# The low part of each weight slot on GpSimd: eight instructions of 256 columns instead of one of 2048

## The chip, the cores and the metric

The kernel runs on one core of one Trainium2 chip. The metric is the device time of one execution in microseconds, the median of three runs. Times inside an execution come from one profiled execution and are given in microseconds from its first instruction.

## What is computed

The reference is a stack of four transformer-like layers over a sequence of 512 tokens with 1024 features, all in float32. Cut to what matters here:

```python
def first_block(x, ...):                       # DEPTH = 2
    h = rms_norm(x, g_mix[0])
    x = x + rwkv7_time_mix(h, ...)             # products with w1, a1, k, r, g1, v, g2, o
    x = x + swiglu_ffn(rms_norm(x, g_ffn[0]), ffn_w_gu[0], ffn_w_down[0])
    k_sh, v_sh = shared_kv(x, kv_g, kv_w, ...)
    x = x + diff_attention(rms_norm(x, g_mix[1]), k_sh, v_sh, ...)
    x = x + swiglu_ffn(rms_norm(x, g_ffn[1]), ffn_w_gu[1], ffn_w_down[1])

def second_block(x, ...):
    x = _even_layer(x, w_in, ..., w_out, ...)  # gated linear attention and spatial gating
    x = _odd_layer(x, w_in, ..., w_out, ...)   # retention and multi-scale pooling
```

The feed-forward part has a gate and up weight of 1024 x 5632 and a down weight of 2816 x 1024 in each of two layers. Together with the projections of the four layers these weights are read once, 143 MB, and every product is computed with the 512 tokens at once.

## The kernel before

**Split products.** A matmul of this kernel takes its operands in a rounded float32 format. To keep float32 precision each operand is split into a high part (the rounded copy) and a low part (original minus high part), and a product is three matmuls: high by high, low by high, high by low (lines 2227, 2228 and 2229, the helper `three`). Activations are in `X_hi` and `X_lo`, eight tiles of 128 x 512.

**Weight slots.** All weights pass through a stream of 135 slots, each of 128 partitions x 2048 columns of float32 (8 tiles of 128 rows by 256 output features; some are smaller). Slot n uses buffer n % 2 of `weight_raw`, `w_hi` and `w_lo`. Four engines hand it on:

- SyncE loads `weight_raw` (1 MB in two DMAs) once the low part of slot n - 2 is made (`lo_ready`).
- ScalarE copies it to `w_hi` (`high`, line 1110), once the DMA has landed (`raw_full`) and TensorE has gone through slot n - 2 (`kstep`), and counts up `hi_ready`.
- GpSimd subtracts: `w_lo = weight_raw - w_hi` (`low`, line 989), and counts up `lo_ready`.
- TensorE waits for `lo_ready` at the first matmul of the slot (`features` and `tokens`). A slot gives 48 matmuls of 128 x 128 by 512 columns.

`regions(n, t)` gives the parts of a slot that hold weights: one part in nearly all, two in slot `g2`, where the first is linked to the second by a wait (`link`). It is two-dimensional for a full slot (`t[:, :]`) and three-dimensional for some narrower ones.

**Order.** Each engine runs its own list of instructions, written out by hand, in order. GpSimd's list is mostly `low` for slot after slot, in the order of the products. In between it has four subtractions for the decay sums of the first layer after each of three `k` slots (line 1017), the level masks of the state solver (lines 1031 and 1038), the gate products of the even layer (line 1050) and the window sums of the odd layer (line 1068). ScalarE's list mixes `high` with the activations, evictions of PSUM and the copies to `X_hi` (line 1128). In the feed-forward loop (`ffn` in each engine's part; two slots an iteration, eleven iterations, for each layer) ScalarE makes the high part of the next slot, then the gate (`Silu`, line 1095), then the high part of the hidden tile (line 1097). VectorE takes the products out of PSUM (lines 1659 and 1660), multiplies them (1663) and makes the low part of the hidden tile (1666).

**VectorE elsewhere.** Around the slots VectorE prepares the activations: `xf` from the normalised state by a scalar product and sum (line 1740), from `x` by a gain (line 1637), and `X_lo = xf - X_hi` (line 1610). Other lines named below: 1802, a running sum along the tokens; 1810, one small scaling; 1961 to 1973, the norm and rotation of queries and keys; 2027 to 2038, the decays of the even layer; 2077, a low part of an inverse norm; 2093, a layer norm's gain; 1696, the subtraction of a mean.

Of the kernel before, what the change touches and what calls it, by code (L numbers as in the profile page):

```python
# [14 lines left out]
F32 = mybir.dt.float32  # L15
# [3 lines left out]
ALU = mybir.AluOpType  # L19
# [196 lines left out]
def step_end(s):  # L216
    return PL.kstart[s + 1]
# [277 lines left out]
def regions(n, t):  # L495

    name = PL.slots[n][0]
    v = t[:, :].rearrange("p (k c) -> p k c", k=8)
    if name in ("a1", "elr"):
        return [v[:, :, 0:128]]  # L500
    if name == "g1":
        return [v[:, :, 0:160]]
    if name == "a2":
        return [t[:, 0:1024]]
    if name == "g2":
        return [t[:, 0:1024], t[96:128, 1024:2048]]
    if name in ("dn0", "dn1") and PL.slots[n][1] % 3 == 2:
        return [v[:, 0:6, :]]
    return [t[:, :]]


def build(nc, t, out):

    JB = make_jobs()
    ctx = ExitStack()
    with ctx:
# [249 lines left out]
        def wait_done(eng, key):  # L766

            eng.wait_ge(job_done, JB.info[key][2] + 1)

        def wait_job(eng, key):  # L770

            _, who, _, n = JB.info[key]
            eng.wait_ge(job_a if who == "A" else job_d, n)
# [6 lines left out]
        def wait_product(eng, name):  # L780
            wait_step(eng, PL.first[name] + PL.count[name] - 1)
# [34 lines left out]
        def whole(tile):  # L816
            return tile[:, :, :, :].rearrange("p b k c -> p (b k) c")

        def mask(name, n=2 * KT):
            at_ = CORE_MASKS.index(name)  # L820
            return lvl[:, at_:at_ + 1, :].to_broadcast([P, n, CH])
# [152 lines left out]
        @block.gpsimd  # L974
        def _(pool):
            seq = [0]

            def link(ins):

                seq[0] += 1  # L980
                ins.then_inc(pool_seq, 1)
                pool.wait_ge(pool_seq, seq[0])

            def low(n, dyn=0):

                pool.wait_ge(hi_ready, n + 1 + dyn)
                parts = list(zip(regions(n, weight_raw[n % 2]), regions(n, w_hi[n % 2]), regions(n, w_lo[n % 2])))
                for i, (r, h, l) in enumerate(parts):
                    ins = pool.tensor_tensor(l, r, h.bitcast(F32), ALU.subtract)  # L989
                    if i < len(parts) - 1:  # L990
                        link(ins)
                ins.then_inc(lo_ready, 1)
                if len(parts) > 1:
                    pool.wait_ge(lo_ready, n + 1)

            def low_product(name):
                for i in range(sum(1 for q in PL.slots if q[0] == name)):
                    low(PL.first_slot[name] + i)

            def low_ffn(layer):  # L1000
                n0 = PL.first_slot[f"gu{layer}"]
                with pool.Fori(0, FT // 2) as i:
                    for j in range(2):
                        low(n0 + j, 2 * i)
                n0 = PL.first_slot[f"dn{layer}"]
                with pool.Fori(0, 2) as i:
                    for j in range(6):
                        low(n0 + j, 6 * i)

            for name in ("a1", "a2"):  # L1010
                low_product(name)
            low(PL.first_slot["k"])
            for i in range(1, 4):
                low(PL.first_slot["k"] + i)
                for k in range(4 * i - 4, min(4 * i, KT)):
                    pool.wait_ge(w_sum, k + 1)
                    pool.tensor_tensor(u0[:, k, :], rf[:, k, :], u0[:, k, :], ALU.subtract).then_inc(w_before, 1)
            for name in ("r", "g1", "v"):
                low_product(name)

            pool.wait_ge(kstep, step_end(PL.first["v"] + 3))
            for i in range(2):
                ins = pool.memset(state[i][:, :, :], 0.0)
            ins.then_inc(zero_ready, 1)
            pool.wait_ge(lvl_in, 16)
            for tt in range(TT):
                wait_job(pool, ("AtX", tt))
                for g in range(2):
                    for slot in range(2):
                        part = TT2[1][:, g, slot, 1, :, :]  # L1030
                        pool.tensor_tensor(part, part, mask("eye", 4), ALU.add).then_inc(f_ready, 1)
                pool.wait_ge(at_copied, tt + 1)
                for lv in range(2, NLV + 1):
                    if lv >= 3:
                        wait_done(pool, ("G", tt, lv - 2, 1))
                    elif tt:
                        wait_done(pool, ("G", tt - 1, 4, 1))
                    pool.tensor_tensor(whole(Lm[(lv + 1) % 2]), whole(At), mask(f"lv{lv}"),
                                       ALU.mult).then_inc(level_ready, 1)
            low_product("g2")  # L1040
            low_product("o")
            low_ffn(0)
            for name in ("q", "kk", "kv", "ao"):
                low_product(name)
            low_ffn(1)
            for name in ("eq", "ek", "elr", "ev", "esv", "eu", "egb", "ega"):
                low_product(name)
            wait_product(pool, "egb")
            for g in range(4):
                pool.tensor_tensor(mix[:, 4 + g, :], mix[:, 4 + g, :], egb[:, g, :], ALU.mult).then_inc(gate_p, 1)  # L1050
            low_product("eo")
            wait_product(pool, "eo")
            pool.memset(opp[:, :, 0:PAD], 0.0).then_inc(pad_p, 1)
            for name in ("oq", "ok", "ov", "op", "ogd"):
                low_product(name)

            pool.wait_ge(pad_p, 1)
            pool.wait_ge(rot_done, 4)
            link(pool.memset(psh[:, :, 0:PAD], 0.0))
            wait_product(pool, "op")  # L1060
            for g in range(4):
                if g >= 1:
                    pool.wait_ge(win_d, g)
                src = opp[:, g, :]
                for i in range(g + 1):
                    dst = psh[:, i % 2, :]
                    sh = 1 << i
                    ins = pool.tensor_tensor(dst[:, PAD:PAD + S], src[:, PAD:PAD + S],
                                             src[:, PAD - sh:PAD - sh + S], ALU.add)
                    if i < g:  # L1070
                        link(ins)
                    src = dst
                ins.then_inc(win_p, 1)
                if g in (1, 3):
                    low(PL.first_slot["ogc"] + g // 2)
            low_product("oo")
# [1811 lines left out]
```

## Time and profile before

| | |
|---|---|
| time, median of 3 runs | 2346.48 us (2332.41 to 2347.68) |
| time of the profiled execution | 2346.41 us |
| its span, first to last instruction | 2344.3 us |
| TensorE busy | 2075.5 us (89%) |
| TensorE weight loads | 1585.3 us (68%) |
| VectorE busy | 838.8 us (36%), 1217 instructions |
| ScalarE busy | 803.3 us (34%), 1043 instructions |
| GpSimd busy | 687.1 us (29%), 198 instructions |
| of it line 989 (`w_lo`) | 605.3 us, 136 instructions |
| read from HBM | 143 MB, mean 63 GB/s |
| mean granted TensorE clock | 0.927 of full speed |

Busy time of an engine counts from the start to the end of its instructions, including time in which an instruction is held. Durations of TensorE's matmuls overlap: while the busy time of one is 0.39 us, the next starts 0.23 us after it at full clock. PE is TensorE, PEld its weight loads, DVE VectorE, ACT ScalarE and POOL GpSimd. A line such as L989 is a line of the kernel.

### The profile page before, as it was taken

The page shows a single profiled execution, that of the slowest core. Times are in us where ns is not written, and L with a number is a line of the kernel's source. Part 1 is how long each engine was busy: PE and PEld are TensorE (multiplying, and loading weights), DVE is VectorE, ACT ScalarE, POOL GpSimd, SP SyncE. Part 2 cuts the span into 40 slices and gives each one's busy share as a digit, 9 for nine tenths or more (in the row PEclk, how much of TensorE's full clock was granted, in tenths as well). Part 3 has the DMA queues.
Part 4 walks back from the last instruction along what each step waited for, and adds up shares of the span by engine and source line. Part 5 has one row for each costly group of instructions (what it writes and reads, how often), then busy time and mean ns, then how long its engine had stood idle before and what let it go on. Part 6 is the DMA issues. An engine that isn't in the chain of part 4 may idle for free.

```text
span 2344.3 us, 36168 instructions
## 1 busy us (share of the span) xinstructions
PE 2075.5 (89%) x15556; PEld 1585.3 (68%) x15556; DVE 838.8 (36%) x1217; ACT 803.3 (34%) x1043; POOL 687.1 (29%) x198
## 2 busy tenths in 40 slices
PE   5979876667999999988997789999998999979997
PEld 2656856653778888866665467888887885747764
DVE  4876153333332221023656633222101234252333
ACT  5663332233244432132124434443212413232232
POOL 0333232201233344423310023334443423203430
PEclk7689999996799999999998789999999998889999
DMA  3112100001123332222210012333322211112110
GB/s 110 36 54 67 41 4 4 4 23 46 54 72 93 104 89 99 99 80 73 68 41 18 1 55 72 95 102 89 99 99 90 90 55 54 36 59 90 54 54 36
DMA packets 190702, 147.06 MB, mean 63 GB/s; under 512 B 6888, under 2 KB 188351, under 8 KB 190576
## 3 DMA queue, kind: packets, MB, share of 16 engines
q1 hardware_dynamic: 190576, 145.18, 20.1%
q8 instruction: 104, 1.70, 0.3%
q14 instruction: 22, 0.18, 0.0%
HBM read 143.06 MB, written 2.10 MB: 62 GB/s over the span
## 4 chain that ended last, share of the span: by engine, by line
PE 77%; DVE 9%; ACT 6%; issue 4%; POOL 2%; DMA 1%; SPq 0%; DVEq 0%; ACTq 0%
PE psum L2227 20%; PE psum L2229 19%; PE psum L2228 19%; PE psum L2376 4%; DVE X_lo L1610 2%; ACT w_hi L1110 1%; PE psum L2303 1%; POOL w_lo L989 1%; DVE xf L1740 1%; PE psum L2233 1%; PE psum L2638 1%; ACT xf L1142 1%; DVE col L2002 1%; PE psum L2601 1%; PE psum L2795 1%
## 5 line engine op out<-in xcount | busy, mean ns | idle before, releaser
L989 POOL TENSOR_TENSOR w_lo<-weight_raw,w_hi 128x2048 fp32r<-128x2048 f32 (+2 forms) x136 | 605.3, 4452 | 1433.3 <-ACT w_hi L1110 1433.1
L2227 PE MATMUL psum<-X_hi,w_hi 128*128 128x512 f32 x1544 | 644.2, 417 | 62.1 <-DVE X_lo L1610 42.5
L2229 PE MATMUL psum<-X_hi,w_lo 128*128 128x512 f32 x1544 | 617.4, 400 | 0.0
L2228 PE MATMUL psum<-X_lo,w_hi 128*128 128x512 f32 x1544 | 617.3, 400 | 0.0
L2227 PEld LDWEIGHTS psum<-X_hi,w_hi 128*128 128x128 f32 x1544 | 299.5, 194 | 181.5 <-issue 95.8
L1110 ACT ACTIVATE w_hi<-weight_raw 128x2048 fp32r<-128x2048 f32 (+2 forms) x136 | 251.7, 1850 | 381.2 <-PE psum L2229 369.8
L2228 PEld LDWEIGHTS psum<-X_lo,w_hi 128*128 128x128 f32 x1544 | 300.2, 194 | 64.6 <-issue 6.7
L2229 PEld LDWEIGHTS psum<-X_hi,w_lo 128*128 128x128 f32 x1544 | 299.3, 194 | 65.9
L1659 DVE TENSOR_TENSOR sgate<-rt,psum 128x512 f32<-128x512 f32 x44 | 30.2, 687 | 320.4 <-PE psum L2229 320.4
L2227 PE MATMUL psum<-hb_hi,w_hi 128*128 128x512 f32 x352 | 136.9, 389 | 0.0
L2228 PE MATMUL psum<-hb_lo,w_hi 128*128 128x512 f32 x352 | 136.9, 389 | 0.0
L2229 PE MATMUL psum<-hb_hi,w_lo 128*128 128x512 f32 x352 | 136.9, 389 | 0.0
L2227 PE MATMUL psum<-w_hi,X_hi 128*128 128x256 f32 x384 | 116.4, 303 | 12.6 <-DVE X_lo L1610 6.5
L1095 ACT ACTIVATE sgate<-sgate 128x512 f32<-128x512 f32 x44 | 27.9, 635 | 255.2 <-DVE sgate L1659 255.2
L2228 PE MATMUL psum<-w_lo,X_hi 128*128 128x256 f32 x384 | 111.0, 289 | 0.0
L2229 PE MATMUL psum<-w_hi,X_lo 128*128 128x256 f32 x384 | 110.9, 289 | 0.0
L1649 DVE TENSOR_TENSOR x<-x,psum 128x512 f32<-128x512 f32 x32 | 20.5, 682 | 224.2 <-PE psum L2229 224.2
L1610 DVE TENSOR_TENSOR X_lo<-xf,X_hi 128x512 fp32r<-128x512 f32 x88 | 76.3, 868 | 50.5 <-ACT X_hi L1128 49.0
L2227 PEld LDWEIGHTS psum<-w_hi,X_hi 128*128 128x128 f32 x384 | 76.3, 199 | 24.8 <-issue 21.8
L2228 PEld LDWEIGHTS psum<-w_lo,X_hi 128*128 128x128 f32 x384 | 76.4, 199 | 2.0 <-issue 1.9
L2229 PEld LDWEIGHTS psum<-w_hi,X_lo 128*128 128x128 f32 x384 | 76.1, 198 | 0.0
L2227 PEld LDWEIGHTS psum<-hb_hi,w_hi 128*128 128x128 f32 x352 | 66.1, 188 | 13.8
(426 smaller groups left out, 2639.2 us busy)
## 6 DMA issues: line engine op xcount, KB each, us to landing
weight_raw<-in_ffn_w_gu SPq DMA_DIRECT2D x88, 512.0 KB, 4.9
weight_raw<-in_l_w_in SPq DMA_DIRECT2D x45, 512.0 KB, 4.6
weight_raw<-in_ffn_w_down SPq DMA_DIRECT2D x40, 512.0 KB, 3.7
weight_raw<-in_kv_w SPq DMA_DIRECT2D x16, 512.0 KB, 4.1
weight_raw<-in_l_w_out SPq DMA_DIRECT2D x16, 512.0 KB, 4.1
weight_raw<-in_rw_w_k SPq DMA_DIRECT2D x8, 512.0 KB, 4.1
weight_raw<-in_rw_w_r SPq DMA_DIRECT2D x8, 512.0 KB, 4.0
weight_raw<-in_rw_w_v SPq DMA_DIRECT2D x8, 512.0 KB, 4.5
```

The costliest lines, as they stand in the source:

```text
L989: ins = pool.tensor_tensor(l, r, h.bitcast(F32), ALU.subtract)
L1095: act.activation(sgate[:, j, :], sgate[:, j, :], ACT.Silu).then_inc(ff_gate, 1)
L1110: last = act.activation(h, r, ACT.Copy)
L1142: act.activation(xf[:, i % 2, :], h_sb[:, k, 1:S + 1], ACT.Copy, scale=omu[:, 8 * mu + k:8 * mu + k + 1]).then_inc(mix_half, 1)
L1610: dve.tensor_tensor(X_lo[:, k, :], f, X_hi[:, k, :].bitcast(F32), ALU.subtract).then_inc(xlo_ready, 1)
L1659: dve.tensor_tensor(sgate[:, j, :], rt[:, :], bank(b[0]), ALU.mult).then_inc(ff_raw, 1)
L1740: return dve.scalar_tensor_tensor(out=f, in0=h_sb[:, k, 0:S], scalar=pcol("rw_mu", 8 * mu + k), in1=f, op0=ALU.mult, op1=ALU.add)
L2002: link(dve.tensor_reduce(col[:, 14:16], psum[:, b:b + 2, 0:N], AX.X, ALU.max))
L2227: pe.matmul(ps, wh, xh, start=start, stop=False, skip_group_check=True)
L2228: pe.matmul(ps, wh, xl, start=False, stop=False, skip_group_check=True)
L2229: return pe.matmul(ps, wl, xh, start=False, stop=stop, skip_group_check=True)
L2376: ins = pe.matmul(out(q, r, k), left(q, r, k), right(q, r, k), start=True, stop=True, skip_group_check=True)
```

## The change

`pieces` cuts a part of a slot: a three-dimensional part into its k tiles (8, or 6 in the last slot of a down product), a two-dimensional one into stretches of 256 columns. `low` goes through the pieces of a part one after the other and writes the same values. There is no wait between pieces, and the signal `lo_ready` is still given by the last instruction of the slot. A full slot has eight instructions of 128 x 256 instead of one of 128 x 2048; the slots of 128 or 160 columns per k tile have eight of that width, and those of 1024 columns four.

```diff
+def pieces(r):
+
+    if len(r.shape) == 3:
+        return [r[:, k:k + 1, :] for k in range(r.shape[1])]
+    return [r[:, c:c + 256] for c in range(0, r.shape[1], 256)]
@@
                 parts = list(zip(regions(n, weight_raw[n % 2]), regions(n, w_hi[n % 2]), regions(n, w_lo[n % 2])))
-                for i, (r, h, l) in enumerate(parts):
-                    ins = pool.tensor_tensor(l, r, h.bitcast(F32), ALU.subtract)
+                for i, part in enumerate(parts):
+                    for r, h, l in zip(*(pieces(q) for q in part)):
+                        ins = pool.tensor_tensor(l, r, h.bitcast(F32), ALU.subtract)
                     if i < len(parts) - 1:
                         link(ins)
                 ins.then_inc(lo_ready, 1)
```

## Rows read from the trace of the kernel before

**Rows 1.** The chain that ended last, shares of the span by line.

```profile
by line: PE psum L2227 20.3%; PE psum L2229 19.1%; PE psum L2228 19.1%; issue 4.2%; PE psum L2376 4.2%; DVE X_lo L1610 2.2%; ACT w_hi L1110 1.4%; PE psum L2303 1.4%; POOL w_lo L989 1.4%; DVE xf L1740 1.3%; PE psum L2233 0.9%; PE psum L2638 
```

**Rows 2.** The chain in order of time: start us, us, what; VectorE pieces.

```profile
146.32 4.50 DVE xf L1740
...
643.15 4.70 DVE X_lo L1610
...
1204.92 4.90 DVE tq L1969
...
1778.81 7.71 DVE X_lo L1610 x6
...
1961.52 2.97 DVE en_lo L2077
...
2072.01 2.35 DVE x L1696
```

**Rows 3.** Timeline, GpSimd and VectorE: start us, us, engine line op out<-in [idle before].

```profile
642.68 4.62 POOL L989 TENSOR_TENSOR w_lo<-weight_raw,w_hi 128x2048 fp32r<-128x2048 f32 x1 [6.29 <-ACT w_hi L1110]
...
1982.93 3.70 DVE L2093 TENSOR_SCALAR esv<-esv,pv 128x512 f32<-128x512 f32 x1
```

**Rows 4.** Waits, 671 to 913 us: waited for, us in total, times, longest us.

```profile
PEld psum L2227 <- POOL w_lo L989: 4.0, 10, 0.4
```

**Rows 5.** Timeline of the first feed-forward product, ScalarE, GpSimd and TensorE.

```profile
710.93 4.60 POOL L989 TENSOR_TENSOR w_lo<-weight_raw,w_hi 128x2048 fp32r<-128x2048 f32 x1 [7.96 <-ACT w_hi L1110]
...
729.67 1.28 ACT L1110 ACT_TABLE_LOAD   x1
730.97 1.92 ACT L1110 ACTIVATE w_hi<-weight_raw 128x2048 fp32r<-128x2048 f32 x1
732.96 4.60 POOL L989 TENSOR_TENSOR w_lo<-weight_raw,w_hi 128x2048 fp32r<-128x2048 f32 x1 [7.96 <-ACT w_hi L1110]
...
737.25 0.39 PE L2229 MATMUL psum<-X_hi,w_lo 128*128 128x512 f32 x1
737.62 0.50 PE L2227 MATMUL psum<-X_hi,w_hi 128*128 128x512 f32 x1
```

**Rows 6.** Timeline of GpSimd: instructions that follow each other, merged with their count.

```profile
102.97 8.69 POOL L1017 TENSOR_TENSOR u<-rf,u 128x512 f32<-128x512 f32 x4
...
252.78 9.04 POOL L989 TENSOR_TENSOR w_lo<-weight_raw,w_hi 128x2048 fp32r<-128x2048 f32 x2 [19.82 <-ACT w_hi L1110]
...
298.30 2.78 POOL L1031 TENSOR_TENSOR TT<-TT,lvl 128x256 f32<-128x256 f32 x4 [3.06 <-DVE TT L1841]
```

**Rows 7.** The chain in order of time: `w_lo`, first and last of seven.

```profile
117.96 4.66 POOL w_lo L989
...
2203.64 4.57 POOL w_lo L989
```

**Rows 8.** Timeline, GpSimd and TensorE: down product, and a slot of 1831.69.

```profile
926.82 4.61 POOL L989 TENSOR_TENSOR w_lo<-weight_raw,w_hi 128x2048 fp32r<-128x2048 f32 x1 [7.81 <-ACT w_hi L1110]
932.78 0.39 PE L2227 MATMUL psum<-hb_hi,w_hi 128*128 128x512 f32 x1
...
1831.69 5.39 POOL L989 TENSOR_TENSOR w_lo<-weight_raw,w_hi 128x2048 fp32r<-128x2048 f32 x1 [7.99 <-ACT w_hi L1110]
```

**Rows 9.** Timeline of TensorE: what ended its idle time, after three stalls.

```profile
1135.30 0.70 PE L2611 MATMUL psum<-aq,cst 128*128 128x512 f32 x1 [0.39 <-DVE aq L1961]
...
1212.10 0.70 PE L2611 MATMUL psum<-ak,cst 128*128 128x512 f32 x1 [1.68 <-DVE ak L1961]
...
1964.53 0.50 PE L2233 MATMUL psum<-en_hi,heads_r 16*128 16x512 f32 x1 [3.58 <-DVE en_lo L2077]
```

**Rows 10.** Stretches: us, busy us by engine (x count), PEclk, DMA share, GB/s.

```profile
120.00:124.00 4.00, 1.64 (x8) 1.06 (x7) 1.11 (x1) 3.54 (x7) 4.00 (x3) 1.00 0.05 14
...
152.00:158.00 6.00, 5.65 (x18) 4.30 (x18) 3.42 (x6) 3.73 (x6) 0.00 (x0) 0.72 0.45 157
...
1966.00:1976.00 10.00, 10.00 (x24) 7.04 (x24) 5.87 (x6) 0.63 (x1) 3.31 (x3) 0.53 0.25 85
```

## The prediction

> **What bounds the kernel now.** I read the chain that ended last by line, then in order of time, then the waits by stretch, and last the timeline of single engines around each place where the chain leaves TensorE. The three matmul lines of the split products alone are 58% of the chain [rows 1], so nothing outside TensorE counts unless TensorE waits for it. Two things that belong to this change do stand on the chain: `w_lo` on GpSimd with 1.4% (33 us, seven pieces of about 4.6 us) and `X_lo` on VectorE with 2.2%, although one `X_lo` takes 0.68 us when it is alone.
>
> The `X_lo` share is a stall by GpSimd. At 146.32, 643.15 and elsewhere on the chain a VectorE operation of 0.5 to 0.75 us lasts 2 to 5 us [rows 2] (the pieces at 229.05 and 1404.49 repeat these two), and each time it ends about 0.55 us after a `w_lo` subtraction does: 643.15 + 4.70 = 647.85 against 642.68 + 4.62 = 647.30 [rows 3]. VectorE operations that read two SBUF tiles are held, and so is one with a column scalar (at 1982.93, 3.70 us for what takes 0.49); those that read PSUM and one SBUF tile are not. In the whole trace some 35 are held, 93 us in all, but only eleven of the long ones are on the chain.
>
> The second reading decides the sign. In each of the two feed-forward products TensorE waits for `w_lo` ten times, 0.40 us at a time on its weight loads [rows 4]. That looks like nothing, but it means that the slack of these twenty slots is already zero. The timeline shows why [rows 5]: in every second step ScalarE comes late to the slot, after the gate and a table load of 1.28 us, and copies the high part until 732.89; GpSimd subtracts from 732.96 to 737.56; and the matmul that needs it starts at 737.62, 0.37 us after its predecessor instead of 0.23. Whatever is added to the subtraction of such a slot is added to the step.
>
> **What the change costs.** It takes out 136 subtractions and puts about eight times as many in their place, with the same columns in sum, no wait between them, and one signal after the last. DMAs, copies and matmuls stay. The price is a start cost for each further instruction. No row shows a subtraction of 256 columns in this line, so I bound it [rows 6]. Two whole slots back to back take 9.04 us, the second 4.57 of it, so their starts are 4.47 apart; four instructions of 256 columns (L1031) take 2.78 us, the last 0.74 of it (0.735), so 0.68 apart. Between the two lie 1792 columns and 3.79 us: 2.11 ns a column and 0.14 us a start. Eight pieces then cost at least what one slot costs now (4.60 us, no start cost at all) and at most 8 x 0.735 = 5.88 us, if they don't overlap in the least (+1.28). Between them I take the row of the same length and no wait between instructions: 7 x 0.68 + 0.74 = 5.50 us, or by the start cost 4.60 + 7 x 0.14 = 5.58; that is +0.95 us a slot.
>
> The Trainium skill (Perfetto Trace Analysis, GPSIMD Engine Instruction) says that the reported span of a GpSimd instruction is unreliable and that start-to-start spacing should be used. By spacing the price is +0.9 to +1.0 and by durations +1.28, which over the 28 slots below is 9 us more; the row of L1031 gives both readings, 0.68 and 0.74.
>
> Where it lies on the path: (a) twenty feed-forward slots, 20 x 0.95 = 19.0 us. (b) The seven `w_lo` on the chain, from 117.96 to 2203.64 [rows 7]: TensorE waits right behind each (behind the last, GpSimd's own window sums, for which TensorE waits), 7 x 0.95 = 6.7; and VectorE may now come in between pieces, one small operation at 174.78 (0.35) and one at 1855.43 (0.45). (c) The slot of 1831.69, which TensorE takes up at once when it ends at 1837.08 [rows 8]: 0.95, and a multiplication (0.55) and a scan (1.08) of VectorE that now come in between, 2.5 in all. Together 29.0 us. The other slots of the feed-forward products are hidden: in the down product 926.82 + 4.61 = 931.43 is first used at 932.78 [rows 8]. This cover of 1.35 us holds at +0.95; beyond 1.35 some ten slots like it cost too. All others have 2 us and more, or a pause of TensorE behind them that is longer than what is added; so have the slots of 97.47 and 129.80, where VectorE is dense and the low part may end 3 to 5 us later than now.
>
> **What it gives back.** I need what happens when both engines want the path. From 102.97 four GpSimd operations of 1.08 us take 8.69 us while VectorE scans of the same length stand in line: strictly in turn, one each [rows 6]. So a held VectorE operation will wait for one piece of 0.54 us, not for eight; but the next one waits for a piece too, until all eight are through. GpSimd needs its 4.3 us of the shared path as before, and only what falls into VectorE's own pauses is won. I laid it out place by place, pieces of 0.54 us in turn with VectorE work of 0.35 (scalar) to 0.62 us. At 146.32 and 229.05, where ScalarE and VectorE hand tiles to each other with a pause of 0.86 us per tile, it wins 1.85 of 3.75 us (3.7 for both). At 643.15 and 1404.49 VectorE is back to back, 0.95 of 4.0 each (1.9). At 1778.81 six `X_lo` in 7.71 us become 6.3 (1.4). At 1961.52 it wins 1.8, at 2072.01 1.3. At 1204.92 the stall is 4.2 us, but TensorE idled only 1.68 behind it [rows 9], so 1.7; at 1129.50 the same bound, from TensorE's pause of 0.39, leaves 0.4. Two places in the first 85 us give 1.0. The sum is 13.2 us. The bounds of this term are nothing (GpSimd keeps the path over all eight) and the stalls less those TensorE bounds, 27.
>
> A clock term comes with 1961.52. TensorE stands still for 3.58 us before 1964.53 [rows 9], and from 1966 to 1976 its granted clock is 0.53, almost all of it the lower level of 1.2 GHz [rows 10]. After the pause of 2.36 us between 120 and 124 the clock stayed at 1.00. With 1.8 us of the 3.58 left I take this dip as gone: 10 x (1 - 0.53) = 4.7 us.
>
> The sum is 29.0 - 13.2 - 4.7 = +11.1 us. The profiled execution took 2346.4 us (span 2344.3) and the median of the runs is 2346.5, so both lead to 2357.5 us.
>
> **The rivals.** First, the other side: the start cost is hidden. Only the last piece is waited for, so GpSimd's cores could run on from piece to piece and end the slot after 4.6 us as now. Then (a) is nothing, of (b) and (c) only VectorE's 2.4 us remain, and the time is 2346.4 + 2.4 - 17.9 = 2331. Nobody waits between the four of L1031 either, and they are 0.68 apart, not 0.54; that speaks against it. It turns to a gain where 28 x + 2.4 falls under 17.9, at x = 0.55 us a slot or 0.08 a start. 12%. (The Trainium skill, GPSIMD Engine Reference, Instruction dispatch, describes this running on: a core takes up the next instruction once its own share is done, and completion holds only what waits on the semaphore. No row of this trace shows it at the end of a piece.)
>
> Second, dearer pieces. At 0.735 each, without overlap, it is 28 x 1.28 + 2.4 - 17.9 = +20, 2366 us. At 0.75 a slot is dearer by 1.4, the cover of the down product is gone, and it is 2370 and more. The duration of L1031 is close to this point, its spacing isn't. 15% for 2370 or more.
>
> Third, GpSimd keeps the path over the eight pieces, for they stand ready in its queue. Then VectorE waits for all eight, 0.95 longer than now at the seven places that TensorE doesn't bound (6.7), wins nothing and never comes in between: 2346.4 + 26.6 + 6.7 = 2380. The turns from 102.97 speak against it, though GpSimd's instructions were twice as long there. 8%.
>
> Fourth, the twenty TensorE pauses of 1.3 us make its clock dip. Between 152 and 158, after a pause of 2.81, it was granted 0.72 [rows 10], which costs 6 x 0.28 = 1.7 us; twenty times that is 34, and the time 2391. But the pause of 2.36 left the clock at 1.00. 4%.
>
> **How the numbers follow.** The forecast (pieces 0.62 to 0.74 us apart, in turn with VectorE) has 58%, with a range of its own from 2345 to 2368. The rivals have 12, 15, 8 and 4%, and 3% are left for what I don't see. The low end of 2338 is half-way to the first rival, the high end of 2378 nearly the third. A measurement of this kernel can tell about 1%, 23 us, from no change. Faster by more needs the hidden start cost and nearly all of VectorE's stalls besides: 4%. Slower by more, above 2370, is rivals two to four less what falls short of it: 25%. Within 1%: 71%.
>
> **What would show it.** In the changed profile: two pieces start 0.68 us apart in the feed-forward loop and a slot takes 5.5 us; TensorE's wait for `w_lo` there is about 1.3 us at each of the twenty slots, and two steps take 23.0 us where they now take 22.03 (710.93 to 732.96, [rows 5]); no `X_lo` takes over 1.3 us; `w_lo` has a larger share of the chain and `X_lo` a smaller one; the clock after 1965 is 1.00. I am wrong if the spacing is under 0.6 or over 0.75, if a VectorE operation still waits 4 us, or if the feed-forward loop doesn't get longer.

## The result and the profile after

| | before | after |
|---|---|---|
| time, median | 2346.48 us (2332.41 to 2348.87, 9 runs) | 2358.21 us (2356.06 to 2363.49, 9 runs) |
| ratio, with its 95% interval | | 1.0067 (1.0049 to 1.0085) |
| profiled execution, its span | 2346.41 us, 2344.3 | 2360.45 us, 2358.3 |

The kernel became slower by 0.5 to 0.85%, which is 11 to 20 us. That is less than the 1% that the prediction took as the bound of "no change". The forecast was 2357.5 us.

The profile's page of the kernel after, engines and the costliest group (busy us, mean ns of one, idle before it):

```profile
PE 2069.8 (88%) x15556; PEld 1585.3 (67%) x15556; DVE 795.1 (34%) x1217; ACT 803.7 (34%) x1043; POOL 853.0 (36%) x1122
...
L997 POOL TENSOR_TENSOR w_lo<-weight_raw,w_hi 128x256 fp32r<-128x256 f32 (+1 forms) x1060 | 774.5, 766 | 1287.0 <-ACT w_hi L1118 1286.9
```

GpSimd went from 605.3 to 774.5 us for the same columns. VectorE is busy 44 us less for the same 1217 instructions (838.8 before): this is held time that has gone, on balance. Line numbers behind the change are higher by 8.

The chain that ended last, by line, to be read against [rows 1]:

```profile
by line: issue 16.9%; POOL w_lo L997 13.0%; PE psum L2235 12.5%; PE psum L2237 11.5%; PE psum L2236 11.5%; PE psum L2384 4.3%; DVE X_lo L1618 1.9%; ACT w_hi L1118 1.5%; DVE xf L1748 1.3%; ACT xf L1150 1.0%; PE psum L2646 0.9%; PE psum L2241
```

`w_lo` went from 1.4 to 13.0%. Most of this isn't new time. As soon as TensorE waits for a slot, the chain is followed back through it, and through what was beside TensorE's work before. The new time is in the waits. From 671 to 930 us (us in total, times, longest), against [rows 4]:

```profile
PEld psum L2235 <- POOL w_lo L997: 13.9, 10, 1.4
PE psum L2235 <- POOL w_lo L997: 9.7, 10, 1.0
```

The two rows are the same ten pauses, seen by the weight load and by the matmul. The weight load waited 0.40 us each before and waits 1.39 now. One of them in the timeline (GpSimd, then TensorE), against [rows 5]:

```profile
731.86 5.59 POOL L997 TENSOR_TENSOR w_lo<-weight_raw,w_hi 128x256 fp32r<-128x256 f32 x8 [7.96 <-ACT w_hi L1118]
...
736.15 0.39 PE L2237 MATMUL psum<-X_hi,w_lo 128*128 128x512 f32 x1
737.51 0.50 PE L2235 MATMUL psum<-X_hi,w_hi 128*128 128x512 f32 x1 [0.97 <-POOL w_lo L997]
```

The eight pieces take 5.59 us where one instruction took 4.60, and the matmul behind them starts 1.36 us after its predecessor instead of 0.37. That is +0.99 us each, twenty times.

On the other side, VectorE against [rows 3] and [rows 2] (643.15, 4.70 us for one `X_lo`):

```profile
640.32 7.97 POOL L997 TENSOR_TENSOR w_lo<-weight_raw,w_hi 128x256 fp32r<-128x256 f32 x8 [5.29 <-ACT w_hi L1118]
...
642.42 1.22 DVE L1618 TENSOR_TENSOR X_lo<-xf,X_hi 128x512 fp32r<-128x512 f32 x1
643.68 0.85 DVE L1645 TENSOR_SCALAR xf<-x,pv 128x512 f32<-128x512 f32 x1
644.45 1.22 DVE L1618 TENSOR_TENSOR X_lo<-xf,X_hi 128x512 fp32r<-128x512 f32 x1
645.71 0.84 DVE L1645 TENSOR_SCALAR xf<-x,pv 128x512 f32<-128x512 f32 x1
```

The 4.70 us are gone. Each `X_lo` waits for one piece (1.22 instead of 0.68 us), and so does each operation behind it, while GpSimd's slot is stretched to 7.97 us. The two engines take turns, one instruction each.

**Where the time went.** TensorE executes the same list in both kernels, so each slot can be matched in two traces. The table gives how much longer each stretch is than in the profile of the kernel before, in us, for all kernels of this study; the stretches are named by their times in before. The two long stretches are the gate and up products. "Held slot" is the stretch of one slot around 1961.52, 22.33 us long before.

| kernel | to 651 | gate, up 1 | 903 to 1413 | gate, up 2 | to 1956 | held slot | next slot | rest | sum |
|---|---|---|---|---|---|---|---|---|---|
| after | -2.3 | +9.4 | +0.1 | +8.9 | +2.8 | -4.9 | +0.2 | -0.1 | +14.0 |
| ffn_only | -0.6 | +9.3 | +0.2 | +8.9 | -1.0 | -0.2 | -6.4 | -1.2 | +9.1 |
| rest_only | +2.5 | +0.1 | -3.2 | -0.1 | +1.0 | -4.8 | +0.2 | 0.0 | -4.3 |
| order | -5.2 | -2.7 | +2.7 | -3.1 | +0.2 | 0.0 | -6.4 | -0.8 | -15.3 |
| order_pieces | +2.4 | -3.5 | -0.1 | -3.9 | +4.3 | -3.3 | -6.4 | -0.8 | -11.3 |
| two | -2.2 | +1.6 | +1.3 | +1.0 | +0.7 | -5.3 | -3.0 | -0.4 | -6.4 |
| sixteen | +5.2 | +26.7 | +0.4 | +28.8 | +9.2 | -3.5 | -3.2 | +1.7 | +65.3 |
| order_four | +2.1 | -3.1 | -0.7 | -3.5 | +3.0 | -6.6 | +0.2 | -0.5 | -9.2 |
| one_slot | +1.1 | 0.0 | 0.0 | 0.0 | +0.2 | -3.3 | -6.4 | -0.5 | -8.9 |

The gate and up columns repeat to 0.1 us between kernels with the same code there (after and ffn_only, before and rest_only or one_slot). The first column doesn't: ffn_only, order and one_slot have the code of before there and differ by 6 us. Nor does "next slot", whose code is the same but for the cut of a slot that has slack: it is -6.4, about -3 or +0.2, and that doesn't go by the cut. One profile is good for the gate and up products, and for single stalls, but not for a sum over the rest. There the kernels have to be compared in two groups: those whose other slots are cut (after, rest_only, order_pieces), and those whose are not (ffn_only, order, one_slot).

### The profile page after: what moved, and what is told of

It reads as the page before. It is cut to its first block, busy times and chain, and to the rows that moved or that the text cites. A ratio compares the mean times of both kernels' runs of the same rounds, so it can differ in the third digit from the quotient of the medians.

```text
span 2358.3 us, 37092 instructions
## 1 busy us (share of the span) xinstructions
PE 2069.8 (88%) x15556; PEld 1585.3 (67%) x15556; DVE 795.1 (34%) x1217; ACT 803.7 (34%) x1043; POOL 853.0 (36%) x1122
## 4 chain that ended last, share of the span: by engine, by line
PE 54%; issue 17%; POOL 13%; DVE 8%; ACT 7%; DMA 1%; SPq 0%; POOLq 0%; DVEq 0%; ACTq 0%
POOL w_lo L997 13%; PE psum L2235 12%; PE psum L2237 12%; PE psum L2236 12%; PE psum L2384 4%; DVE X_lo L1618 2%; ACT w_hi L1118 2%; DVE xf L1748 1%; ACT xf L1150 1%; PE psum L2646 1%; PE psum L2241 1%; DVE col L2010 1%; PE psum L2609 1%; PE psum L2619 1%; PE psum L2311 1%
## 5 line engine op out<-in xcount | busy, mean ns | idle before, releaser
L997 POOL TENSOR_TENSOR w_lo<-weight_raw,w_hi 128x256 fp32r<-128x256 f32 (+1 forms) x1060 | 774.5, 766 | 1287.0 <-ACT w_hi L1118 1286.9
L1618 DVE TENSOR_TENSOR X_lo<-xf,X_hi 128x512 fp32r<-128x512 f32 x88 | 70.1, 797 | 49.3 <-ACT X_hi L1136 48.0
L2237 PEld LDWEIGHTS psum<-hb_hi,w_lo 128*128 128x128 f32 x352 | 66.1, 188 | 13.8
```

Source lines behind the costliest of these rows:

```text
L1618: dve.tensor_tensor(X_lo[:, k, :], f, X_hi[:, k, :].bitcast(F32), ALU.subtract).then_inc(xlo_ready, 1)
L2237: return pe.matmul(ps, wl, xh, start=False, stop=stop, skip_group_check=True)
```

## The experiments

**Which half costs, which half gives.** Theory: the loss sits in the twenty gate and up slots without slack, and the gain in the rest. `ffn_only` cuts the slots of the gate, up and down products alone, `rest_only` all the others. Both use this edit, with `not in` for the second:

```diff
+                    cut = PL.slots[n][0][:2] in ("gu", "dn")
+                    for r, h, l in (zip(*(pieces(q) for q in part)) if cut else [part]):
```

> The pieces are made only in the slots of the two feed-forward products; all other slots keep one subtraction. My theory: the loss sits in the twenty slots where TensorE waits for the low part, at seven further starts of 0.14 us each, so the time is that of before plus 19 to 20 us, about 2366 us, and the loss of each pair of steps is 1.0 us. Rival A: the longer low part does its harm by starting the next weight DMA later, wherever DMAs are dense; then the loss is spread over all products, and this kernel shows 5 to 10 us of it. Rival B: nothing but TensorE's clock differs; then it lies anywhere within 5 us of before.

> The other half: pieces in all slots but those of the feed-forward products. My theory: gains where VectorE was held (13 us) and one lost clock dip (5 us), less the start cost of the eight other slots on the path (10 us), so 8 us under before, about 2338 us. Rival A (later DMAs): at or above before, as there is no gain to be had from VectorE. Rival B: within 5 us of before.

Measured beside a kernel before of 2343.52 us: `ffn_only` 2359.6 us (2355.52 to 2362.47), ratio 1.0081 (1.0055 to 1.0106); `rest_only` 2337.75 us (2333.57 to 2346.68), ratio 0.9971 (0.9953 to 0.9989). In us that is +19.0 (12.9 to 24.8) and -6.8 (-2.6 to -11.0). The two add up to +0.52%, within the interval of the whole change. Both rivals of `ffn_only` are out: neither 5 to 10 us nor anything within 5 us of before lies in its interval. For `rest_only` a loss or nothing (rival A) is out; "within 5 us of before" (rival B) is not, the interval reaches from -2.6 to -11.0. The waits of `ffn_only` from 671 to 930 us are those of after:

```profile
PEld psum L2236 <- POOL w_lo L998: 13.9, 10, 1.4
PE psum L2236 <- POOL w_lo L998: 9.7, 10, 1.0
```

**Is it the missing slack?** If it is, giving these slots slack must take the cost away while all the pieces stay. `order` is the kernel before with ScalarE's list in the feed-forward loop changed: the high part of slot j + 2 comes ahead of the gate of slot j, so that it no longer waits for the gate, the copy of the hidden tile and the table load.

```diff
+                high(n0 + 1)
+                with act.Fori(0, FT // 2 - 1) as i:
...
+                        high(n0 + j + 2, 32 * i, 16 * i)
+                        gate(i, j)
+                high(n0 + FT)
+                for j in range(2):
+                    gate(FT // 2 - 1, j)
```

`gate` is the `Silu` and the copy to `hb_hi`, as before. `order_pieces` is the same on the kernel after.

> The kernel before, with one subtraction a slot, but in the feed-forward loop ScalarE makes the high part of a slot as soon as TensorE has left its buffer, ahead of the gate and the hidden tile, and no longer after them. My theory: TensorE's 0.25 us at every second step goes, 20 x 0.25 = 5 us, about 2341 us, and the low part then has some 4 us to spare in every step. Rival A: nothing changes, as DMAs set the pace; or the gates come too late and it is slower.

> The changed kernel with the same order of ScalarE's work. My theory: with slack in every step the eight pieces cost nothing in the feed-forward products, so their 20 us and the 5 us of the order are gone: 2358 - 25 = 2333 us, 8 us under the order alone. Rival A (later DMAs): the loss of 20 us stays, 2353 us or more. Rival C (pieces cost TensorE by themselves, through its clock or the path to SBUF): likewise above 2345.

Measured: `order` 2337.85 us (2330.62 to 2344.59), ratio 0.9983 (0.9964 to 1.0003); `order_pieces` 2333.07 us (2329.18 to 2336.33), ratio 0.9962 (0.9946 to 0.9978). With the pieces the order is worth 1.05% (1.0067 to 0.9962, each against before on its own chip); without them it can't be told from nothing by the runs, though the two products of its profile are 5.8 us shorter, as expected (5). Both rivals of `order_pieces` are out, since it is under 2345 in every run. It was to be 8 us under `order`; it is 4.8 us by the medians, and the intervals overlap. GpSimd and TensorE of `order_pieces`:

```profile
729.86 6.50 POOL L997 TENSOR_TENSOR w_lo<-weight_raw,w_hi 128x256 fp32r<-128x256 f32 x8 [4.36 <-ACT w_hi L1126]
...
727.66 0.39 PE L2243 MATMUL psum<-X_hi,w_hi 128*128 128x512 f32 x1
727.89 0.39 PE L2244 MATMUL psum<-X_lo,w_hi 128*128 128x512 f32 x1
728.12 0.39 PE L2245 MATMUL psum<-X_hi,w_lo 128*128 128x512 f32 x1
728.34 0.39 PE L2243 MATMUL psum<-X_hi,w_hi 128*128 128x512 f32 x1
```

A slot now takes 6.50 us, longer still, since the pieces have come to lie beside VectorE's work on the hidden tile. It costs nothing. No wait of TensorE for `w_lo` is left from 671 to 913 us, its matmuls stay 0.23 us apart, and both gate and up products are shorter than before (-3.5 and -3.9). `order`, without pieces, has -2.7 and -3.1 there; the 0.8 us between them is what VectorE wins at the start of each product, and in the steps themselves the two kernels are equal. This shows the cause of the loss: the pieces cost 0.99 us a slot or more, but time is lost only where nothing hides it, and that was so in twenty slots.

**How the cost grows with the number of pieces.** `two` has pieces of 1024 columns, `sixteen` of 128:

```diff
-    return [r[:, c:c + 256] for c in range(0, r.shape[1], 256)]
+    return [r[:, c:c + 1024] for c in range(0, r.shape[1], 1024)]
```

> Two pieces of 1024 columns instead of eight of 256. Theory (a start cost of 0.14 us for every further instruction, and strict turns): a slot is 0.14 us dearer, so the twenty feed-forward slots give +2.8 and the other places on the path +1.1; a held VectorE operation waits for at most one piece of 2.2 us instead of 4.5, which wins about 5. Together -1 to -3: 2341 to 2343 against 2343.5 before. Rival (the price of the twenty slots comes from cutting at all, as later signals or later DMAs, and not from the number of pieces): +15 to +19 as with eight, 2355 or more.

> Sixteen pieces of 128 columns. Theory: 15 further starts of 0.14 us, +2.0 to +2.1 us a slot. The twenty zero-slack slots give +40, the ten slots of the down product whose cover is 1.35 us give another +6.5, the other places on the path +16, and VectorE wins back up to 18 (it waits for at most 0.3 us at a time): +45, 2388 against 2343.5, and two feed-forward steps take 24.1 us where before has 22.0. Rival (price independent of the number of pieces): 2358 as with eight. Rival (pieces so short that GpSimd's start cost grows beyond 0.14, pieces over 0.45 us apart): 2400 and more.

Measured beside a kernel before of 2341.94 us: `two` 2342.56 us (2338.21 to 2350.03), ratio 1.0011 (0.9993 to 1.0028); `sixteen` 2410.85 us (2409.07 to 2415.04), ratio 1.0298 (1.0272 to 1.0324). So `two` is no change, where a gain of 1 to 3 us was expected, and `sixteen` costs 64 to 76 us where 45 were expected. Its time is the one that its second rival named (2400 and more), but that rival's mechanism, a start that becomes dearer, is not what the traces show:

The price of a start is about the same over the whole range. In the stretch before the held slot VectorE is nearly idle, and one slot is made in it. Its rows in before, `two`, `order_four`, after and `sixteen` (us, then busy us of PE, PEld, DVE, ACT and POOL, granted clock, DMA share, GB/s):

```profile
1934.29:1956.02 21.73, 21.73 (x71) 11.06 (x70) 2.06 (x3) 11.62 (x15) 4.59 (x1) 1.00 0.15 49
```

```profile
1936.65:1958.38 21.73, 21.73 (x72) 11.07 (x70) 2.06 (x3) 11.63 (x15) 4.72 (x2) 1.00 0.15 49
```

```profile
1932.06:1953.78 21.72, 21.72 (x71) 11.07 (x70) 2.07 (x3) 11.63 (x15) 5.00 (x4) 1.00 0.15 49
```

```profile
1953.10:1974.83 21.73, 21.73 (x71) 11.05 (x70) 2.07 (x3) 11.63 (x15) 5.57 (x8) 1.00 0.15 49
```

```profile
2004.60:2026.32 21.72, 21.72 (x71) 11.06 (x70) 2.06 (x3) 11.63 (x15) 6.71 (x16) 1.00 0.15 49
```

One to sixteen instructions take 4.59, 4.72, 5.00, 5.57 and 6.71 us: 0.13 to 0.14 us for each further start, and sixteen pieces start 0.42 us apart, not over 0.45. The stretch itself is 21.7 us in all five, since here the slot has slack.

What the expectation of `sixteen` missed is, first, a cost that here came only with longer pauses. Its twenty slots make TensorE pause up to 2.9 us (start to start), and 7 of the steps run at a lower clock. Two such steps:

```profile
747.15:760.85 13.70, 11.17 (x49) 8.93 (x48) 2.70 (x4) 3.07 (x3) 9.60 (x22) 1.00 0.30 82
```

```profile
771.73:786.64 14.91, 12.82 (x49) 10.10 (x48) 3.12 (x4) 3.06 (x3) 9.16 (x22) 0.89 0.33 91
```

Both have the 48 matmuls of one slot. The second has the shorter pause (2.48 against 2.92 us) and is longer by 1.2 us, because it was granted 0.89. At equal pauses (13.29 against 14.91 us) a dip costs 1.6 us, seven of them 11. Second, the pieces alone, at a clock of 1.00, cost either 2.1 us (steps of 13.29 us, where before has 11.15) or 2.6 us (steps of 13.71). The 2.1 are the starts, as expected. The other 0.4 come where VectorE's multiplication of the hidden tile, which now meets the end of the slot, gets in between. Such a slot takes 7.16 instead of 6.71 us:

```profile
742.86 7.16 POOL L997 TENSOR_TENSOR w_lo<-weight_raw,w_hi 128x128 fp32r<-128x128 f32 x16 [9.98 <-ACT w_hi L1118]
767.45 6.71 POOL L997 TENSOR_TENSOR w_lo<-weight_raw,w_hi 128x128 fp32r<-128x128 f32 x16 [8.37 <-ACT w_hi L1118]
```

In the down products the cover gave way, and a little earlier than expected: eight slots cost 0.94 to 1.03 us each, 7.7 in all, where ten at 0.65 were put down (part of the columns "903 to 1413" and "to 1956"). The rivals of `two` and `sixteen` that put the price on cutting at all are out. In `two` the gate and up slots cost 0.18 us each in the first product and 0.12 in the second, 3.0 in all.

**Four pieces, with the order.** This joins what the other runs pointed to.

> ScalarE's order in the feed-forward loop changed as before (high part one slot earlier), and four pieces of 512 columns. Theory: with slack in the twenty slots the pieces cost nothing there; the other places on the path pay 8 x 0.42 = 3.4 instead of 7.6, and VectorE, which waits for one piece of 1.1 us at most, wins some 10: with the -5.7 of the order alone, 2330 to 2334, as good as eight pieces (2333) or slightly better. Rival (VectorE only gains when pieces are about as short as its own operations): nothing is won over the order alone, 2338 or more.

`order_four` takes 2329.52 us (2328.14 to 2336.93), ratio 0.9945 (0.9924 to 0.9967), beside 2341.94 us. It has the lowest ratio of the study, and it is faster than before and, by the ratios, than after. Whether four pieces beat eight with the same order (0.9962), or even the order alone (0.9983), is not told apart: the intervals overlap. So the rival (no gain over the order alone) is made unlikely by the median but is not out.

**The clock term by itself.** `one_slot` cuts the one slot that starts at 1959.41 (`cut = n == 116`).

> Only the slot of 1959.41 is cut into eight. Theory of the prediction: the VectorE operation of 1961.52 is held for 0.6 instead of 3 us, TensorE's pause before 1964.5 goes from 3.58 to about 1.8 us, and the granted clock from 1966 to 1976, 0.53 in the kernel before, is 1.00: -1.8 and -4.7 us, both at this place. Rival (the clock dips by itself, at places that move from run to run, whatever the length of this pause): the pause goes to 1.8 us, but the dip stays or shows up at another stall.

A single execution gave 2337.58 us, which says nothing by itself. What it is for is in two stretches. The held slot, and the slot behind it, in before:

```profile
1956.02:1978.35 22.33, 18.75 (x61) 13.44 (x60) 13.82 (x9) 4.14 (x5) 9.90 (x5) 0.77 0.14 47
1978.35:2013.33 34.98, 34.98 (x137) 26.02 (x136) 10.72 (x12) 5.28 (x7) 4.60 (x1) 0.80 0.09 30
```

in `one_slot`:

```profile
1957.33:1976.37 19.04, 17.21 (x61) 12.52 (x60) 11.98 (x9) 4.15 (x5) 10.94 (x12) 0.82 0.17 55
1976.37:2005.00 28.63, 28.63 (x137) 21.20 (x136) 10.71 (x12) 5.28 (x7) 4.60 (x1) 1.00 0.12 37
```

in after:

```profile
1974.83:1992.29 17.46, 15.62 (x62) 11.48 (x60) 11.59 (x9) 4.15 (x5) 10.97 (x12) 0.90 0.18 60
1992.29:2027.44 35.15, 34.97 (x137) 26.06 (x136) 8.25 (x13) 5.29 (x7) 6.14 (x8) 0.81 0.09 30
```

and in `ffn_only`, where both slots are as before:

```profile
1972.87:1995.04 22.17, 18.59 (x61) 13.38 (x60) 13.82 (x9) 4.15 (x5) 9.91 (x5) 0.77 0.14 47
1995.04:2023.67 28.63, 28.63 (x138) 21.20 (x136) 10.71 (x12) 5.28 (x7) 4.60 (x1) 1.00 0.11 37
```

The held slot is 22.2 to 22.3 us wherever it isn't cut and 17.5 or 19.0 where it is in eight. Of the difference 1.75 us are the pause itself (3.97 to 2.22 us, start to start), and 1.5 or 3.1 the clock, 0.82 or 0.90 instead of 0.77. So the dip becomes smaller but doesn't go; the expectation of -4.7 us failed, and its rival is right in that the dip stays. The 6.4 us of the next slot come and go by themselves: 28.63 us at 1.00 in `ffn_only` and `one_slot`, 35 us at 0.80 in before and after. They must not be credited to any edit (about 3 us in `two` and `sixteen`, at 0.89), and they are a large part of the low sums of single profiles (`one_slot`, `order`). `order_four`, with four pieces, is the one case in which the held slot ran at 1.00 throughout (15.70 us), and then its next slot took 35.17 us.

## Why the prediction was right, and where it was off

- **Start cost.** 0.14 us a start from [rows 6], 5.50 to 5.58 us a slot: measured 5.57 in a quiet stretch, 5.59 in the feed-forward loop (+0.99, not +0.95). The price of no overlap, 1.28, did not come. The duration of a piece (0.736 us) would have misled; the spacing in the feed-forward loop, (5.59 - 0.736) / 7 = 0.69 us, did not. The Trainium skill (Perfetto Trace Analysis, GPSIMD Engine Instruction) says to go by the spacing; the trace agrees, 0.69 against 0.736.
- **(a) The twenty slots without slack, 19.0 us.** Right. Two steps take 23.06 us (12.18 + 10.88) where they took 22.03, and 1.0 us longer in the second product too; together 20 us. In `order_pieces`, where the same pieces have slack, nothing of it is left. This decided the sign. It was read from a wait of 0.40 us with ten occurrences [rows 4], a row far down the list.
- **(b), (c).** Right where they stand alone: the slot of 1831.69 [rows 8] went from 5.39 to 7.78 us, +2.39, forecast 2.5, and TensorE lost 2.3 us there in all three kernels with such pieces, nothing in the others; at 1855.43 it lost 1.4 us (forecast 1.4), at 2203.64 0.9 (0.95). Too low in the first layer: the slot of 117.96 [rows 7] went from 4.66 to 6.62, +1.96, where 0.95 was put down, because VectorE comes in between there too, and the slot of 97.47, put at nothing, now keeps TensorE waiting (0.9 to 1.4 us lost from 104 to 120). Too low also where two slots follow each other at once, as 2110.44 and 2114.91: both are waited for, +2.1 instead of 0.95, with a part that is the clock. The slot of 1797.56 isn't told apart.
- **What VectorE gets back, 13.2 us.** The mechanism is as forecast. No `X_lo` takes over 1.23 us. Places that can be read: 0.77 and 0.81 us at the start of the two gate and up products (forecast 0.95 each), 1.75 at 1204.92 (1.7), 0.45 at 1129.50 (0.4), 1.75 at 1961.52 (1.8). Six `X_lo` at 1778.81 take 6.54 instead of 7.71 us, 1.2 (1.4), but no gain of TensorE is seen behind them: the end of the slot that follows moves by 0.0, -1.2 and +0.4 us in the three kernels. The places at 146 and 229 us can't be read one by one. From 104 to 260 us, which holds both and the slots of 117.96, 174.78 and 252.78, the prediction has 3.2 of cost and 3.7 of gain, -0.5 in sum. Measured are +2.8, +2.7 and +2.4 in the three kernels with pieces there, against +0.5, +0.1 and +1.6 in the three without. So the forecast of this stretch was 2 to 3 us too low, and how much of that is the clock isn't separated.
- **The clock term, -4.7 us.** This step failed: "I take this dip as gone". The dip only shrank, by 3.1 us in after and 1.5 in `one_slot`, and the sign "the clock after 1965 is 1.00" was not met: the held slot ran at 0.90 and the next one at 0.81. The step rested on one row, the clock of 1.00 after the pause of 2.36 us between 120 and 124 [rows 10]. That row doesn't repeat. `one_slot` has the code of before there and a pause of 2.27 us, and was granted 0.88; the stretch to 146 us is 1.5 us longer for it. In `ffn_only`, again with the same code, the pause is 2.77 us and the clock stayed at 1.00. The row of `one_slot`, to be read against the first of [rows 10]:

```profile
120.00:124.00 4.00, 1.73 (x6) 1.10 (x6) 0.83 (x1) 3.26 (x7) 4.00 (x3) 0.88 0.01 3
```

- **The sum.** Its parts were 19.0 for the twenty slots and -7.9 for the rest (10.0 of cost, 13.2 from VectorE, 4.7 from the clock). Measured: `ffn_only` +19.0 by its ratio, `rest_only` -6.8, with intervals of 4 to 6 us to each side. By the median of the whole change it is +11.7 us against a forecast of +11.1, by the ratio +15.7 (11.5 to 19.9). The first part is a hit of the mechanism. The hit on the sum to 1 us is luck in part: the clock gave back less than forecast at 1961.52, the costs in the first layer were too low, and the next slot alone moves single executions by 6.4 us.
- **The rivals.** A hidden start cost falls with the five rows of a quiet stretch. (The Trainium skill, GPSIMD Engine Reference, Instruction dispatch, has a core run on to the next instruction once its own share is done; if that happens here, it still leaves 0.14 us a start.) Dearer pieces fall with 5.59 us. GpSimd keeping the path over all eight falls with the turns at 640.32. The clock rival (pauses of 1.3 us make the clock dip) falls for eight pieces: all twenty steps of the loop ran at 1.00. In `sixteen`, with pauses of 2.5 to 2.9 us, it came true in 7 of 18 steps.

## What to carry to other kernels

Look for the waits that are short and come often. A wait of 0.4 us at every second slot said here that the slack was zero, and everything added upstream of it was paid in full. Give such a slot slack first (here one reordering of ScalarE's list): the edit that cost 0.7% alone costs nothing then, and the two together are at -0.4%. Cutting an instruction of one engine that holds a path shared with another cost a fixed start per piece and shortened the other engine's wait to one piece; but it also let that engine in between, so a slot that is itself waited for grew by 2.0 or 2.4 us instead of 1.0. So cut only as fine as the wait needs, and only where the stalled engine is on the path.

## What the runs showed of the hardware

- A further GpSimd subtraction costs 0.13 to 0.14 us, whether it has 128 or 1024 columns (4.59, 4.72, 5.00, 5.57 and 6.71 us for 1, 2, 4, 8 and 16 pieces).
- GpSimd and VectorE took turns, one instruction each, although GpSimd's pieces stood ready in its queue: an `X_lo` on two SBUF tiles waits for one piece of 256 columns (1.22 instead of 0.68 us; 4.70 beside one of 2048), and GpSimd's pieces wait for VectorE in return (7.97 us for eight instead of 5.59). A VectorE operation that reads PSUM and one SBUF tile isn't held: line 1667 takes 0.69 us beside the pieces as alone.
- A held VectorE operation can be free. In `order` one multiplication of the hidden tile is held in every step, 3.9 us instead of 0.69, 81.5 us in one product, and the product is still 2.7 us shorter than before:

```profile
L1671 DVE TENSOR_TENSOR xf<-sgate,xf 128x512 f32<-128x512 f32 x21 | 81.5, 3879 | 36.7 <-ACT sgate L1094 36.5
```

- TensorE's granted clock after a pause isn't decided by its length alone. With pauses of 1.36 us (start to start) none of twenty steps dipped, with 2.48 to 2.95 us 7 of 18 did, after one of 2.22 us the same slot was granted 0.90 or 0.82, between 120 and 124 us the clock stayed at 1.00 after idle times of 2.36 and 2.77 us and fell after one of 2.27, and one stretch of identical code took 28.6 us at 1.00 or 35 us at 0.80. What else decides it these runs don't show.
